# A two-layer decoder trunk on eight cores: the third block build in pieces, bf16 norm sums, a last pass in two halves, finer norm rows, and more weight buffers and bf16 weight copies

## What is computed

```python
for i in range(2):                                   # BATCH 2, SEQ 8192, D 2048, D_FF 5632
    h = rmsnorm(x, norm[i])
    if i == 0:                                       # mixer A
        gb, gc, xs = split(h @ a_in)                 # 2048 -> 3*2048
        x = x + (gb * conv3(gc * xs)) @ a_out
    else:                                            # mixer B, chunks of 128 positions
        u, v = split(gelu(h @ b_in)); v = rmsnorm(v)
        x = x + (u * (tril(w_s) @ v + b_s)) @ b_out
    h = rmsnorm(x, f_norm[i])
    up = conv3(h @ f_up) + bias                      # 2048 -> 2*5632, causal depthwise conv
    g, a = split(up)
    x = x + (silu(g) * a) @ f_down                   # 5632 -> 2048
return rmsnorm(x, final_norm)
```

## Time and profile before

| | |
|---|---|
| median of 3 runs | 5739.7 us (5373.37 to 5871.24) |
| profiled execution | 5371.17 us |
| its span on the slowest core (core 3) | 5369.6 us |
| spans of the eight cores | 5326.7 to 5369.6 us |
| PE busy | 5101.9 us, 95% |
| DVE, POOL, ACT busy | 2620.7 us, 1963.1 us, 1673.5 us |
| mean granted TensorE clock, core 3 | 0.979 |

### The profile page before, as it was taken

One profiled execution on the slowest core, in us unless ns is written; L12 is line 12 of the kernel. 1 busy time (PEld: TensorE's weight loads), 2 busy tenths in 40 slices (PEclk: granted clock), 3 DMA queues, 4 the chain that ended last, 5 costly groups with the idle time before them and its releaser, 6 DMA issues.

```text
span 5369.6 us, 98237 instructions; the slowest of 8 cores (5326.7 to 5369.6 us)
## 1 busy us (share of the span) xinstructions
PE 5101.9 (95%) x35040; PEld 3422.3 (64%) x35040; DVE 2620.7 (49%) x3610; ACT 1673.5 (31%) x3146; POOL 1963.1 (37%) x1820
## 2 busy tenths in 40 slices
PE   6999999699999999999999998969999999999997
PEld 4666666466666666666677677746666666666665
DVE  4433325667777777110124234566777777711112
ACT  3211111245555555100013223224555555500000
POOL 0000013467777777211110201046677677611111
PEclk8999999899999999999999999989999999999998
DMA  6333238578655544746553636547763233375764
GB/s 164 56 60 60 44 113 257 168 113 130 117 100 114 103 98 100 273 163 231 188 189 128 202 128 220 163 150 121 122 118 69 59 64 69 98 254 180 261 216 160
DMA packets 192210, 754.89 MB, mean 141 GB/s; under 512 B 21872, under 2 KB 56176, under 8 KB 158448
## 3 DMA queue, kind: packets, MB, share of 16 engines
q0 software_dynamic: 33472, 205.59, 23.2%
q1 hardware_dynamic: 117648, 276.62, 15.7%
q10 hardware_dynamic: 40608, 266.41, 14.7%
HBM read 821.04 MB, written 204.32 MB: 191 GB/s over the span
## 4 chain that ended last, share of the span: by engine, by line
PE 62%; DVE 11%; DMA 9%; POOL 8%; issue 6%; ACT 2%; SPq 0%; DVEq 0%; POOLq 0%; ACTq 0%
PE ps L223 62%; POOL X L243 4%; DVE Tg L246 3%; DVE wA L243 3%; POOL mo L243 3%; DMA xl<-xs 2%; DMA wB<-f_up 2%; DMA xb<-xs 1%; POOL s L243 1%; DMA xb<-xh 1%; DVE h L246 1%; ACT Tg L240 1%; DMA xw<-xa 1%; DMA mq<-mo 1%; ACT s L240 1%
## 5 line engine op out<-in xcount | busy, mean ns | idle before, releaser
L223 PE MATMUL ps<-h,wA 128*128 128x344 bf16 x14784 | 2206.9, 311 | 117.8 <-ACT s L240 92.8
L223 PEld LDWEIGHTS ps<-h,wA 128*128 128x128 bf16 x14784 | 1438.9, 98 | 885.7 <-issue 182.2
L223 PE MATMUL ps<-mB,wD 128*128 128x342 bf16 x8360 | 1217.8, 309 | 1.0 <-DMA wD<-wdn 1.0
L223 PEld LDWEIGHTS ps<-mB,wD 128*128 128x128 bf16 x8360 | 819.3, 98 | 400.0 <-issue 2.5
L243 POOL TENSOR_TENSOR acc<-acc,sq 128x684 f32<-128x684 f32 (+5 forms) x180 | 302.3, 1680 | 1906.1 <-ACT sq L240 1906.1
L223 PE MATMUL ps<-hA,wa 128*128 128x343 bf16 (+2 forms) x4560 | 679.1, 312 | 21.7 <-DVE hA L246 20.9
L243 DVE TENSOR_TENSOR xb<-xb,ps 128x684 f32<-128x684 f32 (+4 forms) x208 | 156.7, 755 | 953.8 <-PE ps L223 738.1
L223 PEld LDWEIGHTS ps<-hA,wa 128*128 128x128 bf16 x4560 | 448.3, 98 | 250.5 <-issue 23.3
L243 POOL TENSOR_TENSOR X<-X,c 128x344 f32<-128x344 f32 x528 | 544.0, 1030 | 114.1 <-POOL X L243 94.2
L240 ACT ACTIVATE sq<-xb 128x684 f32<-128x684 f32 (+5 forms) x165 | 127.6, 773 | 1286.2 <-DVE xb L243 1225.3
L246 DVE SCALAR_TENSOR_TENSOR Ta<-ps,cst,Ta 128x684 f32<-128x684 f32 x528 | 478.3, 927 | 49.0 <-ACT Ta L240 19.4
(11 more groups left out here) (72 smaller groups left out, 3556.1 us busy)
## 6 DMA issues: line engine op xcount, KB each, us to landing
wD<-wdn ACTq DMA_DIRECT2D x96, 1408.0 KB, 7.4
wb<-wb ACTq DMA_DIRECT2D x72, 1024.0 KB, 5.8
mq<-mo SPq DMA_DIRECT2D x264, 171.0 KB, 6.1
wA<-f_up POOLq DMA_DIRECT2D x88, 512.0 KB, 6.1
wB<-f_up POOLq DMA_DIRECT2D x88, 512.0 KB, 8.5
wdn<-f_dn POOLq DMA_DIRECT2D x32, 1408.0 KB, 20.9
mB<-mq SPq DMA_DIRECT2D x24, 1197.0 KB, 14.7
xb<-xs SPq DMA_DIRECT2D x80, 342.0 KB, 7.1
```

Of the source, the lines that this page charges most:

```text
L223: ins = e.matmul(bk(bank, col0, col0 + n), l, r, start=(start and i == 0), stop=(stop and i == m - 1), skip_group_check=not start)
```

## The change

- **Third build in pieces.** `h_build(..., fine=True)` cuts each of the 8 steps into three entries (first normalisation, second normalisation, sums), and `f_up` pumps one entry at five places inside a set (and one more at the end of set 0). The sums go "dddpp" instead of "dppdp". Build 1 of each layer gets "dddpp" instead of "ddddd". In the first unit pair the sets go p 0, 1 for type 0, p 0, 1 for type 1, then p 2.
- **bf16 norm sums.** The last POOL addition of a pass writes `accb` in bf16, and `stat_fin` multiplies it by `ones16`; `ones32` is gone.
- **Last pass in two.** In the last `f_down` the third T is split into two passes of 342 positions, so `wD` is loaded 64 times instead of 48. `fin_ops` loads three steps ahead and also covers the first half; only the second half stays in SBUF.
- **Way in row by row.** `h4` takes one row, `each` and `fill` spread rows between the parts of units, and unit (0, 1) is written in the `fine` form, in which each matmul waits for its own row only.
- **More places and copies.** `wo` has 7 slots in passes 0 and 1 (3 in pass 2). The first two units of each layer's f_up are converted once to bf16 in DRAM (`wu16`, during mixer A's way in) and loaded by SP. Unit 0 is loaded and combined in an earlier pass in layer 0. `b_h(2)` moves from the end of B's second input stage to its start.

```diff
-    def stat_add(first, src, srck, n, sq, acc):
-        if first:
+    def stat_add(i, src, srck, n, sq, acc, accb):
+        if i == NCH - 1:
+            act(sq[:, 0:n], src, AF.Square, srck, sq.k(0, n))
+            tt("pool", accb[:, 0:n], acc[:, 0:n], sq[:, 0:n], ALU.add, acc.k(0, n) + sq.k(0, n), accb.k(0, n))
+        elif i == 0:
             act(acc[:, 0:n], src, AF.Square, srck, acc.k(0, n))
...
-            mm(b, c1 - c0, [(ones32[:, :], acc[:, c0:c1])], acc.k(c0, c1) + ones32.k(0, 128))
+            mm(b, c1 - c0, [(ones16[:, :], acc[:, c0:c1])], acc.k(c0, c1) + ones16.k(0, 128))
...
+            each = [lambda part: some(ts, 2), lambda part: some(ts, 2) if part == 2 else some(th, 2),
+                    lambda part: some(th, 4 - part)][max(k, 0)]
+            a_unit(j, v, each, fine=(j, v) == (0, 1), fill=(lambda: some(th, 2)) if k > 0 else None)
...
+        elif j < 15:
+            cast(wu_d[j - 11], f_up_d[(j - 11) // 2 * 2 * NQ + (j - 11) % 2], ("wu", j - 11))
...
+        if fine:
+            works = []
+            for kk in range(8):
+                works += [lambda kk=kk: mul(kk, kk, 0), lambda kk=kk: mul(kk, kk + 8, 2), lambda kk=kk: sums(kk)]
...
+        if u < 2:
+            src, eng, rk = wu_d[2 * l + u], "sp", [("wu", 2 * l + u)]
+        else:
+            src, eng, rk = f_up_d[l * 2 * NQ + u], "pool", []
...
+            pump(0 if late else 1)
             s.prod(s.bA, 6, 2, False)
             s.into(s.bA, "s4")
+            pump(0 if late else 1)
             s.prod(s.bC, 5, 0, False)
...
-            pump(2)
+            pump(2 if idx == 0 else 1)
...
+        PS = [(0, 0, 2), (1, 0, 2)] + ([(2, 0, 2)] if last_x is None else [(2, 0, 1), (2, 1, 1)])
+        NS = NCH * len(PS)
...
-    wslot, wissue = ring_plan(seq, 3)
+    wslot = [0, 1, 2, 3, 4, 5, 6, 0] + [0, 6, 5, 4, 3, 2, 1, 0] + [0, 1, 2, 0, 1, 2, 0, 1]
+    wissue = {0: (3, 3), 1: (4, 4), 2: (5, 5), 3: (6, 6), 4: (7, 0), 8: (0, 0), 16: (3, 0), 17: (4, 1), 18: (5, 2), 19: (6, 0), 20: (7, 1)}
...
+                bg.extend(b_h(2, A0 + 38528, xl2))
+                pump(1)
...
-            if T == 1:
-                bg.extend(b_h(2, A0 + 38528, xl2))
-                pump(1)
...
-        bg.extend(h_build(fup_h(2), 2, si, gcol, fup["xl"] + fup["Tg"][4:6], False, "dppdp"))
+        bg.extend(h_build(fup_h(2), 2, si, gcol, fup["xl"] + fup["Tg"][4:6], False, "dddpp", True))
```

More of the change, by code:

```diff
@@ L357, in a_norm @@
         return ([lambda: sqa(0), lambda: sqa(1), lambda: both(0), lambda: both(1), lambda: sqb(2), lambda: sqb(3)],
-                [lambda g=g: h4(g) for g in range(4)])
+                [lambda c=c: h4(c) for c in range(NCH)])
     bg = deque()
@@ L379, in build_program, with a_unit @@
     ytile = {}
-    def a_unit(j, w, each=None, fine=False):
+    def a_unit(j, w, each=None, fine=False, fill=None):
         t0, n = AWIN[w]
@@ L403, in a_unit @@
                 if each:
-                    each(2 if part == 2 else 1)
+                    each(part)
         t1, t2, t3 = [ring("tmp", tmps) for _ in range(3)]
@@ L431, in build_program, with some @@
         f()
-    todo = deque()
-    def each(k):
-        for _ in range(k):
-            if todo:
-                todo.popleft()()
+    ts, th = deque(), deque()
+    def some(q, k):
+        for _ in range(min(k, len(q))):
+            q.popleft()()
     for w in range(1, 6):
@@ L441, in build_program @@
             sqs, hs = a_norm(w + 1)
-            todo.extend(sqs + hs)
-        for j, v in ([(0, 1), (1, 1), (2, 0), (2, 1)] if w == 1 else [(j, w) for j in range(3)]):
-            a_unit(j, v, each)
+            ts.extend(sqs)
+            th.extend(hs)
+        units = [(0, 1), (1, 1), (2, 0), (2, 1)] if w == 1 else [(j, w) for j in range(3)]
+        for i, (j, v) in enumerate(units):
+            k = i - (len(units) - 3)
+            each = [lambda part: some(ts, 2), lambda part: some(ts, 2) if part == 2 else some(th, 2),
+                    lambda part: some(th, 4 - part)][max(k, 0)]
+            a_unit(j, v, each, fine=(j, v) == (0, 1), fill=(lambda: some(th, 2)) if k > 0 else None)
+            if (j, v) == (0, 1):
+                some(ts, 2)
             if w == 5:
                 load_wa(j + 3)
-        each(99)
+        some(ts, 99)
+        some(th, 99)
     PZ = A0 + 77056
@@ L489, in fetch, with mul @@
                 load(b, z0, n, xs_d[si][:, c, t0 + z0:t1], reads=xkeys(si, c, t0 + z0, t1))
+        def mul(kk, c, w0):
+            b = got[c]
+            if zero:
+                for w in range(2):
+                    o, ok = blk(w0 + w, kk), bkey(w0 + w, kk)
+                    z = 2 if w == 0 else 0
+                    stt(o[:, z:N], b[:, w * NN + z:w * NN + N], cc(gcol + c), R[:, t0 + w * NN + z:t0 + w * NN + N], ALU.mult, ALU.mult,
+                        b.k(0, n) + R.k(t0 + w * NN + z, t0 + w * NN + N) + CK, ok)
+                    if z:
+                        S.op("dve", lambda e, o=o: e.memset(o[:, 0:2], 0.0), writes=ok)
+            else:
+                stt(hv[:, w0:w0 + 2, kk, :], pairs(b, 0), cc(gcol + c), pairs(R, t0), ALU.mult, ALU.mult,
+                    b.k(0, n) + R.k(t0, t0 + NN + N) + CK, bkey(w0, kk) + bkey(w0 + 1, kk))
@@ L506, in f, with first, more @@
-                for i, (o, u, v, op) in enumerate(((4, 0, 3, ALU.add), (6, 0, 2, ALU.add), (5, 1, 3, ALU.add),
-                                                   (2, 2, 3, ALU.subtract), (1, 1, 0, ALU.subtract))):
-                    tt({"d": "dve", "p": "pool"}[engs[i]], blk(o, kk), blk(u, kk), blk(v, kk), op, bkey(u, kk) + bkey(v, kk), bkey(o, kk))
-            return f
+                mul(kk, kk, 0)
+                mul(kk, kk + 8, 2)
+                sums(kk)
+            return f
+        if fine:
+            works = []
+            for kk in range(8):
+                works += [lambda kk=kk: mul(kk, kk, 0), lambda kk=kk: mul(kk, kk + 8, 2), lambda kk=kk: sums(kk)]
+            d = len(xlb) // 2
+            def first():
+                for kk in range(d):
+                    fetch(kk)
+            def more(i):
+                works[i]()
+                if i % 3 == 1 and i // 3 + d < 8:
+                    fetch(i // 3 + d)
+            return [first] + [lambda i=i: more(i) for i in range(24)]
@@ L559, in proj @@
             if i == NCH - 1:
[L560 removed]
+                late.append(lambda: (stat_fin(accb, n, a), after_c(T, -1)))
             after_c(T, i)
[L563 to L580 removed]
     ZF = A0 + 115584
@@ L700, in f_up @@
             if q == 0:
-                sets += [(q, ty, p) for p in range(3) for ty in range(2)]
+                sets += [(q, ty, p) for ps_ in ((0, 1), (2,)) for ty in range(2) for p in ps_]
             elif q == NQ - 1:
@@ L838, in f_down @@
         for n in range(NS):
-            p, c = n // NCH, n % NCH
+            T, c = n // NCH, n % NCH
+            p, w0, nw = PS[T]
+            final = last_x is not None and T == len(PS) - 1
+            s, wd = FS[p] + w0 * NN, nw * NN
             w = fdn["w", n]
             b = 2 * (n % 4)
-            for h in range(2):
+            for h in range(nw):
                 if n == 0 and h == 0:
```

204 lines of the change are left out of this document (92 added, 112 removed).

## The result

The changed kernel took 5312.9, 5313.5 and 5316.7 us; the kernel before 5373.4 and 5381.6 in the executions to compare with.

The account below looks back on a forecast made before the run. PE, busy 95% of the span, was taken as the bound, losing time to waits and the lower clock behind them; 19 + 11 + 14 + 8 + 8 + 18 + 12 + 9 = 99 us off 5371.2 gave 5272 us, range 5245 to 5300.

Parts of the forecast that it names:

- the halved last pass: Third T of last FFN down: weight loads at 345 GB/s lose 13 us, between 0 and 24; second half fits.
- The way in: Mixer A's way in: row-by-row start and three shorter hA waits, with clock, gain 19 us, between 11 and 24.
- the fourth rival: Way in: hA's last row still comes after each unit, 14 us missing, 5286 us; no chance of its own.
- B's third way out: Mixer B, third way out: waits and clock shrink as f_up's conversion goes, 12 us, between 0 and 20.
- A's way out: Mixer A, third pass: emptier queues and no wait for wB at DVE's head, 14 us; 0 if engines stay full.
- B's second way out: Mixer B: b_h(2) moved earlier removes the 10.91 us wait before T 2, with clock 18 us, between 11 and 23.
- The bf16 sums: stat_fin: two bf16 matmuls instead of four f32 in 12 norm sums, 11 us, between 8 and 16.
- The first sets: Start of each FFN up: DVE's waiting for POOL inside a step goes, 8 us per layer, between 0 and 16.
- The last pass's old wait and its clock: Last pass: loads three steps ahead remove the 5.4 us POOL wait, with some 4 us of clock, 9 us.
- the queues and DVE stay full: Way-out and first-set terms (14 + 8 + 8 + 12) give nothing, other terms stay: 5314 us; chance 0.22.
- Everything clears: Whole kernel: waits shrink below what lowers the clock, terms go towards upper bounds: 5231 us; chance 0.25.
- the halved pass: Rival, last pass: becomes a stretch of transfers, a net loss below 226 GB/s; 5412 us at 200; chance 0.03.

Follow-up runs that it names:

- e2: Changed kernel with the fin_ops of the second T not issued, so its output is not written; halving and 64 weight loads stay: 5299.4 us.
- e6: Changed kernel with the first two units of every f_up loaded as f32 and converted by POOL again: B's third way out 90.4 us, A's 238.4.
- e4: Changed kernel with the norm sums in f32 again, stat_fin multiplying by f32 ones: 5353.6 us.
- e5: Changed kernel with the third build in whole steps, two at the end of each set, sums still dddpp: 5353.3 us.
- e1: Changed kernel with its last pass whole again, 48 weight loads, fin_ops still three steps ahead: 5313.6, 5307.7 and 5310.3 us, 0.9858 of before.
- e9: Changed kernel with the third build in whole steps and the builds' sums split between DVE and POOL as before the change: 5377.4 us.
- e7: Changed kernel with b_h(2) put back behind mixer B's second way out: that way out 88.0 us, the third input stage 168.3.
- e10: Changed kernel with the last pass whole and the first unit of every way-in window row by row: 5315.7 and 5320.2 us, 0.984 of before.

## Why the forecast was 40 us off, and what of it held

**The step that failed** is the term of the halved last pass: "I take 345 GB/s ... 115.6 us, a loss of 13 us, between 0 and 24", and after it "the second half fits at all three rates". Measured were 34 us in both halves, where 13 were forecast. The first half lost 21 (123.7 us against 102.4), which is inside the bounds, and the second, costed at nothing, lost 13 (115.4 against 102.3).

For the first half the rate was too high. It moved 300 GB/s as a mean of the cores (290 to 312) at a DMA share of 0.94, below the lowest of the three rates. At 300 GB/s its 39.9 MB would take 133 us; it took 124, so by this estimate some 3 MB were moved later, in the second half. The three rates of the earlier trace rows were the slowest core's, in stretches of 10 to 20 us. In the stretch with 316 the eight cores moved 300 to 316, mean 307, with full engines, and that is the rate that came. In the stretch with 411 the other cores moved 161 to 325, core 0 with full engines only 249. And the earlier trace rows had a longer stretch, 85 us at a share of 0.94 with 269 GB/s, although with converting loads among its transfers.

For the second half the path was wrong: what the first half leaves over, the late `xb` and the lower clock reach into it. Of the "end 13" against "weights 13" that were to cancel, the end gave 9.5 to 10.5 and the weights took 34: some 24 of the missing us, which are 50 by the means over the cores (99 forecast, 49 measured) and 40 by the slowest core. It was not the slots: e2 has the same 64 loads and waits for none.

The page "HBM Reference" of the Trainium skill, in its specifications, gives an effective 358 GB/s per core. By it the first half would have taken 111 us, an estimate; it took 123.7, and no core moved more than 312 GB/s over it.

**The way in** (forecast 19, measured 5.8) failed on a count: "nine rows of 0.5 us ... in front of the last unit's first DVE operation and one behind it, 5 us in a unit whose 48 matmuls take 7" looked at the last unit alone; over both units DVE needs 15.7 us against PE's 14.2. So 2.6 of each 3.1 us stayed. In the first window 11.6 us became 3.9, and the 48 matmuls then took 9.1. That window gave all there was: by the 176th matmul of the units PE is 6.3 us ahead of the kernel before, as a mean (5 forecast), and by the end of the stage 5.8. The three waits and their clock, 14 forecast, gave nothing. That is the fourth rival, named at 14 us less, and it came true at 13.

**B's third way out** (forecast 12, measured 4): PE still waits 5.09 and 2.21 us for `xb` and 1.95 for POOL:

```profile
3463.67 18.98 PE L222 MATMUL ps<-ug,wb 128*128 128x384 bf16 x128 [5.09 <-DVE xb L242]
3484.86 2.49 PE L222 MATMUL ps<-h,wA 128*128 128x344 bf16 x16 [2.21 <-DVE xb L242]
...
3491.06 0.43 PE L222 MATMUL ps<-accb,onesb 128*128 128x322 bf16 x2 [1.95 <-POOL accb L242]
```

The conversion of f_up was one of several users of the queues, and its going was worth 6 to 9 us (e6), of which other parts took back some.

**What held:** A's way out, 14 forecast and 14 measured, but this is luck in good part: DVE's waits for `wB` went as said, yet the copies, the reason given, carry a third of it at most, and the rest has no shown cause. B's second way out, 18 forecast, 17 measured, less 2 to 4 in the input stage, which I had costed at nothing. The bf16 sums, 11 forecast, fit the some 10 of e4 without being shown by them; there are 13 such sums, with 26 matmuls, and not 12 with 24, since the halved pass adds one. The first sets, 8 in each layer: the FFN ups gave 13.5 and 7.1 where both kernels ran together, a norm sum and the waits of units 2 and 3 among them; set 4 came 42.9 us after the first normalisation where 45 were worked out, through the step named (DVE's waiting for POOL inside a step), and whole steps do nearly as well (e5). From the last matmul of the chunks to the end are the 22 us forecast, but the gain is 9.5 to 10.5 and not 13: the 35.2 it was taken from is the slowest core's, and the mean before was 32.4. The last pass's old wait and its clock, 9: e1 has 651.9 us for FFN down and end together against 660.6, 8.7 less.

The page "SBUF — State Buffer" of the Trainium skill, on the two sides of the memory, would have made the normalisations cheaper with fewer sums on POOL. They did not become so: in the first layer the 16 of the build took 1.22 us each in the changed kernel, against 1.24 before and 1.25 in e9 with the old split, and in the second 1.37, against 1.26 and 1.29. The gain was in the sums and in the waits before them.

Of the rivals, "the queues and DVE stay full" gave 5314, the time that came out, but by luck: the terms that it sets to nothing did pay, and others fell short. "Everything clears" is excluded by the waits that stayed; the halved pass never came near 226 GB/s, the point at which it would have turned the whole change into a loss, but it did turn into a stretch of transfers and is a loss by itself, 34 us against the 9.5 it gives.

## What to carry to other kernels

Cost a heavier load of weights by the rate that all cores reach in the same stretch, as long a one as there is, and not by one core's best short one; add what arrives late behind it. Where an engine has more work than its partner between two points, both orders tried here left the wait (3.1 and 2.6 us), and a finer wait removed it. And give the sums of one step to the engine that reads them next: here eight more sums on DVE cost no time, and 6 us of waits between the engines went.

## What was not expected of the hardware

- With all eight cores at this load, each moved 290 to 312 GB/s over 119 to 128 us, at a DMA share of 0.93 to 0.96, and PE waited; without `fin_ops` they moved 279 to 285 at 0.84 to 0.90 over 102 us, and PE did not wait in it.
- With full DMA engines the rates differ widely: in one stretch of 10 us (4690 to 4700 in the kernel before) one core moved 411 GB/s and two others, at shares of 1.02 and 1.01, moved 249 and 296.
- The same kernel's first FFN up takes 1141.8 us at one time and 1154.9 at another, the kernel before 1158.2 and 1168.4; among three kernels that ran together on one chip and hardly differ there (e6, e7, e10) it still ranged from 1154.6 to 1162.7. The cause is open.
- 24 sums of 128 x 344 in bf16 on DVE took 11.0 us, and 16 with two of five on POOL between them 12.1: three in a row took 1.29 us, single ones beside POOL's 0.86 and 0.88.
